# A two-block transformer kernel: where VectorE scales the probabilities of an attention unit, and how far behind its scores a unit is turned

## What is computed

```python
# sparse attention: 8 heads in 2 key groups, query tiles of 128, here for each of two key sets
# (selected blocks ks/vs, sliding window kw/vw; with 512 tokens both see all causal keys)
ss = einsum('bqgjd,bqgnkd->bgjqnk', qb, kg) * scale
ss = where(valid_s, ss, NEG_INF)
ps = softmax(ss, axis=-1)
o_s = einsum('bgjqnk,bqgnkd->bqgjd', ps, vg)
...
o = gb[..., 0:1] * o_c + gb[..., 1:2] * o_s + gb[..., 2:3] * o_w   # o_c: compressed blocks

# dilated attention: 3 dilation groups, 4 heads, joined by one softmax over the three
s = where(valid, einsum(q, k) * scale, NEG_INF); m = max(s); e = exp(s - m); den = sum(e)
o = einsum(e, v) / den;  alpha = softmax(m + log(den)) over the groups;  o = sum(alpha * o)
```

## Time and profile before

| | |
|---|---|
| median of three runs | 3739.39 us (3737.88 to 3741.65) |
| profiled execution, its own time | 3744.49 us |
| its span, from the first to the last instruction | 3743.2 us |
| busy: TensorE, VectorE, ScalarE, GpSimd | 94%, 58%, 41%, 13% of the span |
| mean granted TensorE clock | 0.975 of full speed |
| sparse attention with its projections | 1919.7 to 2141.6 us of the span |
| dilated attention with its projection | 2171.2 to 2294.1 us of the span |

### The profile page before, as it was taken

One profiled execution on the slowest core, in us unless ns is written; L12 is line 12 of the kernel. 1 busy time (PEld: TensorE's weight loads), 2 busy tenths in 40 slices (PEclk: granted clock), 3 DMA queues, 4 the chain that ended last, 5 costly groups with the idle time before them and its releaser, 6 DMA issues. The chain is left out here.

```text
span 3743.2 us, 49705 instructions
## 1 busy us (share of the span) xinstructions
PE 3532.9 (94%) x20631; PEld 2958.0 (79%) x20631; DVE 2177.3 (58%) x3635; ACT 1522.7 (41%) x2254; POOL 486.5 (13%) x427
## 2 busy tenths in 40 slices
PE   7998999999989988999998999999999998999999
PEld 5755678888876557887666677799989998898899
DVE  3275472333374746444645435379999975666666
ACT  3245542221224464222454534333576764333322
POOL 0000000000000000000000021003332344343340
PEclk9999999999999999999998999999999998999999
DMA  6400112333212002222221153247777889988884
GB/s 250 161 6 1 57 49 101 122 124 113 102 46 82 1 23 79 101 92 100 106 74 51 58 161 116 92 159 270 263 264 265 292 321 343 329 322 312 325 322 160
DMA packets 123666, 581.56 MB, mean 155 GB/s; under 512 B 14080, under 2 KB 31600, under 8 KB 82480
## 3 DMA queue, kind: packets, MB, share of 16 engines
q1 hardware_dynamic: 67744, 365.46, 27.2%
q0 software_dynamic: 55696, 212.91, 16.1%
HBM read 516.97 MB, written 61.34 MB: 154 GB/s over the span
## 5 line engine op out<-in xcount | busy, mean ns | idle before, releaser
L538 DVE TENSOR_TENSOR WL<-stage,WH 128x2048 fp32r<-128x2048 f32 x239 | 546.1, 2285 | 345.7 <-ACT WH L528 345.7
L667 PE MATMUL ps<-HH,WH 128*128 128x512 f32 (+1 forms) x1672 | 620.3, 371 | 23.0 <-DVE HL L993 16.2
L528 ACT ACTIVATE WH<-stage 128x2048 fp32r<-128x2048 f32 x239 | 455.2, 1905 | 391.7 <-PE ps L669 350.1
L668 PE MATMUL ps<-HL,WH 128*128 128x512 f32 (+1 forms) x1672 | 612.0, 366 | 0.0
L669 PE MATMUL ps<-HH,WL 128*128 128x512 f32 (+1 forms) x1672 | 608.8, 364 | 0.0
L667 PE MATMUL ps<-HP,WH 128*128 128x384 f32 (+1 forms) x1088 | 381.0, 350 | 13.8 <-DVE WL L538 12.7
L667 PEld LDWEIGHTS ps<-HH,WH 128*128 128x128 f32 x1672 | 317.6, 190 | 92.0 <-issue 29.9
L668 PE MATMUL ps<-LP,WH 128*128 128x384 f32 (+1 forms) x1088 | 374.2, 344 | 0.0
L669 PE MATMUL ps<-HP,WL 128*128 128x384 f32 (+1 forms) x1088 | 373.7, 343 | 0.0
L669 PEld LDWEIGHTS ps<-HH,WL 128*128 128x128 f32 x1672 | 317.0, 190 | 53.7
L668 PEld LDWEIGHTS ps<-HL,WH 128*128 128x128 f32 x1672 | 317.5, 190 | 50.5 <-issue 1.2
(11 more groups left out here) (479 smaller groups left out, 5744.8 us busy)
## 6 DMA issues: line engine op xcount, KB each, us to landing
stage<-in_w SPq DMA_DIRECT2D x64, 1024.0 KB, 4.8
stage<-in_u SPq DMA_DIRECT2D x64, 1024.0 KB, 5.9
stage<-in_v SPq DMA_DIRECT2D x64, 1024.0 KB, 6.9
stage<-in_w_mod SPq DMA_DIRECT2D x40, 1024.0 KB, 4.8
adram<-GA SPq DMA_DIRECT2D x128, 192.0 KB, 7.0
gdram<-GST SPq DMA_DIRECT2D x24, 1024.0 KB, 10.0
GR<-gdram POOLq DMA_DIRECT2D x32, 768.0 KB, 8.1
AR<-adram POOLq DMA_DIRECT2D x32, 768.0 KB, 9.5
```

Source lines behind the costliest of these rows:

```text
L528: act.e.activation(k.WH[o % 2][:, 0:w], k.stage[n % 2][:, 0:w], ACT.Copy).then_inc(*act.done("slab_hi", n))
L538: dve.e.tensor_tensor(k.WL[o % 2][:, 0:w], k.stage[n % 2][:, 0:w], k.WH[o % 2][:, 0:w].bitcast(F32), ALU.subtract).then_inc(*dve.done("sla ...
L667: pe.e.matmul(o, wh[:, kk, cs], L.view(L.hh, kk, z), start=first, stop=False)
L668: pe.e.matmul(o, wh[:, kk, cs], L.view(L.hl, kk, z), start=False, stop=False)
```

## The change

VectorE's scaling of a unit becomes a step of its own, `weigh`. In both attentions the piece of unit n holds the `weigh` of unit n-1 behind the scores of n; the last unit is weighed in the first piece of the tail. In the sparse attention a unit is turned three units behind its scores in place of two, and its values follow four behind in place of three; in the dilated attention a unit is still turned two behind. The instructions themselves are the same.

```diff
--- before.py
+++ after.py
@@ -2203,10 +2203,12 @@
     scored, turned = [], []
     for n, (qt, c, j) in enumerate(units):
         piece = []
-        if len(scored) == 2:
+        if len(scored) == 3:
             piece.append(("turn", scored[0]))
             turned.append(scored.pop(0))
         piece.append(("scores", (qt, c, j)))
+        if scored:
+            piece.append(("weigh", scored[-1]))
         scored.append((qt, c, j))
         if len(turned) == 2:
             piece.append(("values", turned.pop(0)))
@@ -2217,8 +2219,9 @@
         if (c, j) == (2, 1) and qt < 3:
             piece.append(("block_turn", qt + 1))
         yield piece
+    last = [("weigh", units[-1])]
     while scored or turned:
-        piece = []
+        piece, last = last, []
         if scored:
             piece.append(("turn", scored[0]))
             turned.append(scored.pop(0))
@@ -2355,7 +2358,7 @@
             for b in range(2 * nb):
                 mm = pe.e.transpose(p[:, 128 * b:128 * b + 128], pb[:, 128 * b:128 * b + 128], k.ident[:, :])
             mm.then_inc(*pe.done("nt_mm", u))
-        else:
+        elif kind == "values":
             qt, c, j = u
             nb, ptc, ptb = qt + 1, k.PTC.of(qt), k.NPTb.of(u)
             if j == 0:
@@ -2458,6 +2461,9 @@
             i.then_inc(*dve.done("ns_max", u))
             dve.wait_ge("ns_max", u)
             dve.e.tensor_scalar(m[:, 2:4], m[:, 0:2], -1.0, None, ALU.mult).then_inc(*dve.done("ns_negmax", u))
+        elif kind == "weigh":
+            qt, c, j = u
+            Lk, pb, m = 128 * (qt + 1), k.NPb.of(u), k.nsms.of(u)
             dve.wait_ge("ns_exp", u)
             dve.e.reciprocal(m[:, 6:8], m[:, 4:6]).then_inc(*dve.done("ns_recip", u))
             dve.wait_ge("ns_recip", u)
@@ -2482,13 +2488,16 @@
             piece.append(("turn", scored[0]))
             turned.append(scored.pop(0))
         piece.append(("scores", u))
+        if scored:
+            piece.append(("weigh", scored[-1]))
         scored.append(u)
         if len(turned) == 3:
             piece.append(("values", turned[0][0:2]))
             del turned[0:2]
         yield piece
+    last = [("weigh", u)]
     while scored or turned:
-        piece = []
+        piece, last = last, []
         if scored:
             piece.append(("turn", scored[0]))
             turned.append(scored.pop(0))
@@ -2627,6 +2636,8 @@
 
 def vector_dil(k, dve, piece):
     for kind, u in piece:
+        if kind == "weigh":
+            vector_dil_weigh(k, dve, u)
         if kind != "scores":
             continue
         p = k.psw.of(("ds", u))
@@ -2642,10 +2653,14 @@
         dve.wait_ge("ds_max", u)
         dve.wait_ge("ds_max2", u)
         dve.e.tensor_scalar(m[:, 3:4], m[:, 0:1], m[:, 1:2], -1.0, ALU.max, ALU.mult).then_inc(*dve.done("ds_negmax", u))
-        dve.wait_ge("ds_exp", u)
-        dve.e.reciprocal(m[:, 2:3], m[:, 1:2]).then_inc(*dve.done("ds_recip", u))
-        dve.wait_ge("ds_recip", u)
-        dve.e.tensor_scalar(pb[:, :], pb[:, :], m[:, 2:3], None, ALU.mult).then_inc(*dve.done("ds_ready", u))
+
+
+def vector_dil_weigh(k, dve, u):
+    pb, m = k.DPb.of(u), k.dsms.of(u)
+    dve.wait_ge("ds_exp", u)
+    dve.e.reciprocal(m[:, 2:3], m[:, 1:2]).then_inc(*dve.done("ds_recip", u))
+    dve.wait_ge("ds_recip", u)
+    dve.e.tensor_scalar(pb[:, :], pb[:, :], m[:, 2:3], None, ALU.mult).then_inc(*dve.done("ds_ready", u))
 
 
 
```

## The result

Medians: 3761.63 us (3757.26 to 3770.42, 6 runs) against 3740.52 us for the kernel before, measured beside it (3737.88 to 3742.89, 6 runs). The ratio is 1.0057, its 95% interval 1.0047 to 1.0067. The forecast was 3760, range 3745 to 3769.

A forecast was written before the change was run, and what follows sets the result against it. TensorE was taken to bound both stretches. -0.5 sparse + 8.4 + 2.4 + 2.5 + 8.0 = +20.8 us on the profiled 3744.5 gives 3765.3; less 5.1 to the median, 3760 us, range 3745 to 3769.

The forecast's parts named there:

- Second turns: Dilated two-piece chunks: second turn waits for scaling behind the new maximum; net 2.1 us in four chunks, 8.4 us.
- The last one: Dilated chunk with the last scores and turn 14, no scores behind it: its late turn costs 2.4 us.
- The first turn: Start of dilated stretch: unit 0 scaled only after unit 1's maximum, turn 0 late; 2.5 us, between 2.0 and 3.5.
- Sparse stretch: Sparse attention: four terms, 1.6 - 0.9 - 0.4 - 0.9, about -0.5 us; bounds -5 to +5 us.
- the late copies: Sparse second pieces: turns still wait for ScalarE's copy behind rope work; values moved out of six stalls cost +1.6 us.
- the relief at the tail: Sparse tail: a turn that came later now fills the 3.3 us stall before the values; 0.9 us won.
- the earlier block scores: Sparse, where block scores follow: VectorE starts their chain earlier; 0.9 us won, 0.4 in the query tile before.
- The clock: Dilated stretch: TensorE's clock falls after five new gaps, 1.6 us each, 8.0 us; ends 0 and 15.
- Faster: Rival, both stretches: VectorE freed of exponential waits, TensorE's stalls on VectorE go; -16 us, 3723 us; chance 0.09.
- no effect: Rival: scaling is ready before TensorE asks for the turn, only VectorE's idle time shifts; 3739 us; chance 0.07.
- sparse hurt: Rival: accumulator held across a projection makes some twelve sparse chunks wait about 1 us more; +12, 3772 us; chance 0.07.
- slower without the clock: Rival, dilated stretch: new gaps come but are too short to cost the clock; +12.8, 3752 us; chance 0.15.

The follow-up runs named there:

- dilated_only: The changed kernel with the sparse attention put back as before, so only the dilated part of the change is left: 3762.05 us, ratio 1.0055 to the kernel before.
- sparse_only: The changed kernel with the dilated attention put back as before, so only the sparse part is left: 3738.3 us, ratio 0.9998 to the kernel before.
- filled: The changed kernel with two unread TensorE products ahead of each of the five late dilated turns: 3752.97 us, ratio 1.0038 to the kernel before.
- dil_three: The changed kernel with dilated units turned three units behind their scores in place of two: 3737.12 us, ratio 0.9988 to the kernel before.
- weigh_first: The changed kernel with the dilated scaling of unit n-1 put ahead of the scores of n: 3738.83 us, ratio 0.9996 to the kernel before.

## Why the prediction was right

The direction, the place, and the size came out of the steps of the prediction. Against its own profiled execution it said +20.8 us; the profiled one gave +16.3, the medians +21.1. In the profiled execution the terms of the dilated stretch add up to its growth of 16.8 us: 2.7 at the start, 10.0 for the five late turns, and 4.1 for the clock, where the forecast had 2.5, 10.8 and 8.0. The path and the waits were right. That the median came within 2 us of the forecast is in part luck: the clock term changes from one execution to the next, 4.1 us in the profile of the kernel after and 10.3 us in that of `dilated_only`.

- **Second turns.** Forecast: 2.44 us late, net 2.1 each. Measured: scaling to turn as forecast (2.27 us of idle time; from the scaling's end, 2242.36, to the turn it is 0.14 us, the estimate was 0.15). From the first turn of the chunk to the second scores it is 5.09 us (2238.19 to 2243.28) where it was 3.18: net 1.91. Four times that is 7.6 in place of 8.4. I had the reciprocal start at the end of the negated maximum, and it starts 0.13 us behind the start of it (2241.42, 2241.55); and from this turn to the scores it is 0.78 us, where I had 0.88.
- **The last one.** 2.4 forecast, 2.34 measured.
- **The first turn.** 2.5 forecast, within 2.0 to 3.5. The third scores start at 2195.58 in place of 2191.58, and the stretch started 0.8 us later, so 3.2. Part of that comes back: from the first scores to the first turn of the first two-piece chunk it is 66.13 us in place of 63.39, so 2.7. From the negated maximum to the third scores it is 2.53 us (2193.05 to 2195.58), of which 1.44 is the turn on the slow clock, where I had 0.84. The other 0.6 us is not the change's own: the slab split L538 starts 1.4 us later than before, 0.6 beyond the late start of the stretch, since ScalarE's write-out ahead of it waited 22.38 us for its output transfer where it was 21.75. The same wait is 21.1 to 23.0 us in the other kernels, with no pattern that follows the change.
- **Sparse stretch.** -0.5 forecast (its four terms make -0.6). It keeps its length: it starts 0.8 us later in the profiled execution and ends 0.8 us later (first dilated scores 2172.06, before 2171.27). By the medians of `sparse_only` the part is -1.7 us, and its interval holds zero. TensorE's idle time there fell by 0.4 us. I had the kind of the late copies right and the relief at the tail about right (1.2 us, forecast 0.9). Of the 1.3 us for the earlier block scores the last query tile gave 0.4: its two waits of 0.54 and 1.37 us became one of 1.50. The other tile gave 0.5 us, but before its block turn, and its later waits got 0.2 us longer. The waits for the maximum before the scores grew instead.
- **The clock.** 8.0 forecast by a mean over three gaps; `filled` puts it at 7.2 to 8.6. In the profiled execution the half speed lasted 10.2 us in two pieces and cost 4.1 us. That alone does not put this execution below its median by much (0.9 us); most of the 4.8 us between +16.3 and +21.1 is the profiled execution of the kernel before. In that of `dilated_only` the clock fell behind four of five gaps, in 23.9 us of half speed, which cost 10.3 us by the same distances between turns, and from the first scores to the last turn it takes 7.0 us longer than the kernel after (143.5 and 136.4 us). The window behind its second gap (columns as in the earlier trace rows); in the kernel after the clock stayed up behind this gap:

```profile
2253.07:2259.87 6.80, 6.79 (x39) 5.08 (x40) 1.95 (x7) 2.53 (x7) 0.00 (x0) 0.55 0.00 0
```

  The Trainium skill, "TensorE: Matmul & The Clock Gate", section on how the oscillation bites in real kernels, would have these gaps cost no clock; the traces disagree, in part: two of the five gaps of 2.27 us cost it in the kernel after, four in `dilated_only`. Its account of what a drop costs, half of the time spent at the low clock, is a little more than they show: 4.1 of 10.2 us, and 10.3 of 23.9.
- **Rivals.** Faster and no effect fall with `dilated_only`; sparse hurt falls with `sparse_only`; slower without the clock (3752) is what `filled` shows by construction: 3753.0. The granted clock of the dilated stretch fell to 0.93, where the forecast had about 0.9.
- **What I did not see.** The argument against the faster rival was right for this order of work, but for a narrower reason than I gave. VectorE's waits cost nothing as long as ScalarE's roots hold the copies. With those out of the way, and the turns three behind, the later scaling is worth 17.5 us.

## What to carry to other kernels

To move a step behind the next unit's work lengthens its way to its reader by one unit; the reader has to move by one unit too, or the wait comes back on the engine that bounds (`dil_three`); or the step goes ahead of the next unit's work and not behind it (`weigh_first`). Look at places where two pieces follow each other without filler work between them: there the depth counts, and in the others it is hidden. A change that gives nothing may still be the right one, once the wait in front of it is gone; try the two together.

## What the runs showed of the hardware

- Gaps of the same length at the same place in the program cost the clock in one execution and not in another: of the five 2.27 us gaps, two in the kernel after and four in `dilated_only`. The two executions differ by 6.2 us in this stretch for that alone. The gap of 2.55 us before the turn at 2110, or 2.77 us with the new sparse order, kept the clock in the profiles of all nine kernels in which it stood. A shorter one, 2.13 us before the values at 2135, lost it in all six in which it stood. So the length of a gap alone does not decide; what does is open, and nothing was tried for it.
- Work that nobody reads, two products in each of five gaps, saved 7 to 9 us by the medians: the granted clock stayed at 2.4 GHz behind the five gaps.
